# Recurrent mixer of a two-block network: the last pooled tile turned among the last head's units, output tiles in another order, decays and states placed among the running sums, and the opening's row sums moved up

## What the reference computes, cut to what matters

```python
def hgrn2_mixer(q_in, f_in, i_in, g_in, lb, norm_g):
    log_f = logaddexp(log(lbh), log1p(-lbh) + log_sigmoid(z)); k = (1 - lbh) * sigmoid(-z)
    o = hgrn2_chunkwise(q, k, v, log_f)      # S_t = diag(f_t) S_{t-1} + k_t outer v_t, o_t = S_t^T q_t
    o = o * rsqrt(mean(o * o, axis=-1) + EPS) * norm_g
    return o.reshape(B, T, D_A) * silu(g_in)

o_a = hgrn2_mixer(q_a, f_a, i_a, g_a, lb_all[l], hgrn_norm[l])       # features 0 to 511
o_b = multiscale_pool(u_b, pool_w[l], pool_scale[l])                 # features 512 to 1023
x = x + concatenate([o_a, o_b], axis=-1) @ w_out[l]
```

## Time and profile before

| | |
|---|---|
| Time, median of 3 runs | 3008.76 us (3006.59 to 3009.8) |
| The profiled execution, its own time | 3008.41 us |
| Its span in the trace | 3006.6 us |
| TensorE busy in the span | 2968.4 us (99%) |
| VectorE, ScalarE, GpSimd busy | 1636.9, 1124.9, 71.8 us |
| Recurrence of the mixer, layer 1 and layer 2 | 1222.9 to 1289.4 us and 2351.6 to 2417.4 us |

### The profile page before, as it was taken

One profiled execution on the slowest core, in us unless ns is written; L12 is line 12 of the kernel. 1 busy time (PEld: TensorE's weight loads), 2 busy tenths in 40 slices (PEclk: granted clock), 3 DMA queues, 4 the chain that ended last, 5 costly groups with the idle time before them and its releaser, 6 DMA issues.

```text
span 3006.6 us, 33005 instructions
## 1 busy us (share of the span) xinstructions
PE 2968.4 (99%) x14050; PEld 2420.9 (81%) x14050; DVE 1636.9 (54%) x1869; ACT 1124.9 (37%) x1341; POOL 71.8 (2%) x84
## 2 busy tenths in 40 slices
PE   8999999999999999999999999999999999999998
PEld 6786877878888888878788888888888878788886
DVE  5656555565545564654545446545564654545445
ACT  5536445454222235434422223222235434422222
POOL 0000000000000000300000000000000300000000
PEclk9999999999999999999999999999999999999999
DMA  4121221212233232023122222222232014222221
GB/s 157 43 93 55 88 95 43 84 65 97 98 116 111 89 115 98 29 71 140 71 98 98 90 93 98 98 101 96 92 119 98 29 71 140 70 98 98 91 92 69
DMA packets 41922, 270.51 MB, mean 90 GB/s; under 512 B 5776, under 2 KB 6032, under 8 KB 10544
## 3 DMA queue, kind: packets, MB, share of 16 engines
q1 hardware_dynamic: 41776, 268.40, 25.4%
HBM read 266.22 MB, written 2.10 MB: 89 GB/s over the span
## 4 chain that ended last, share of the span: by engine, by line
PE 87%; DVE 7%; ACT 5%; issue 1%; DVEq 0%; POOL 0%; DMA 0%; ACTq 0%; SPq 0%; POOLq 0%
PE PS L257 26%; PE PS L259 25%; PE PS L258 25%; DVE w_lo L231 4%; ACT w_hi L223 3%; DVE XT L1560 2%; PE PS L2175 1%; PE PS L635 1%; PE PS L1149 1%; PE PS L1177 1%; PE PS L2435 1%; PE PS L2466 1%; PE PS L694 0%; PE PS L996 0%; PE PS L2155 0%
## 5 line engine op out<-in xcount | busy, mean ns | idle before, releaser
L223 ACT ACTIVATE w_hi<-w_raw 128x2048 fp32r<-128x2048 f32 x241 | 461.2, 1914 | 1156.8 <-PE PS L259 1156.5
L231 DVE TENSOR_TENSOR w_lo<-w_raw,w_hi 128x2048 fp32r<-128x2048 f32 x239 | 547.7, 2292 | 398.1 <-ACT w_hi L223 397.2
L257 PE MATMUL PS<-uh_b,w_hi 128*128 128x512 f32 x1312 | 511.7, 390 | 0.0
L259 PE MATMUL PS<-uh_b,w_lo 128*128 128x512 f32 x1312 | 510.6, 389 | 0.0
L258 PE MATMUL PS<-ul_b,w_hi 128*128 128x512 f32 x1312 | 510.5, 389 | 0.0
L257 PE MATMUL PS<-uh_a,w_hi 128*128 128x512 f32 x864 | 341.3, 395 | 4.2 <-DVE XT L548 3.4
L258 PE MATMUL PS<-ul_a,w_hi 128*128 128x512 f32 x864 | 336.9, 390 | 0.0
L259 PE MATMUL PS<-uh_a,w_lo 128*128 128x512 f32 x864 | 336.9, 390 | 0.0
L259 PEld LDWEIGHTS PS<-uh_b,w_lo 128*128 128x128 f32 x1312 | 246.2, 188 | 51.3
L257 PEld LDWEIGHTS PS<-uh_b,w_hi 128*128 128x128 f32 x1312 | 246.3, 188 | 51.0
L258 PEld LDWEIGHTS PS<-ul_b,w_hi 128*128 128x128 f32 x1312 | 246.3, 188 | 50.7
(11 more groups left out here) (334 smaller groups left out, 3679.4 us busy)
## 6 DMA issues: line engine op xcount, KB each, us to landing
w_raw<-in_weights SPq DMA_DIRECT2D x241, 1024.0 KB, 4.8
XT<-in_xT SPq DMA_DIRECT2D x8, 256.0 KB, 5.6
mem_raw<-in_mem SPq DMA_DIRECT2D x2, 1024.0 KB, 4.8
out<-XT SPq DMA_DIRECT2D x8, 256.0 KB, 2.0
bands<-in_bands SPq DMA_DIRECT2D x2, 768.0 KB, 6.2
mask_numbers<-in_masks SPq DMA_DIRECT2D x1, 1152.0 KB, 7.6
w_raw<-in_weights SPq DMA_DIRECT2D x4, 256.0 KB, 4.4
p_raw<-in_pT SPq DMA_DIRECT2D x2, 512.0 KB, 3.5
```

The costliest lines, as they stand in the source:

```text
L223: act.activation(self.hi[g % 2][:], self.raw[g % 2][:], ACT.Copy).then_inc(self.hi_done.sem, 1)
L231: dve.tensor_tensor(self.lo[g % 2][:], self.raw[g % 2][:], self.hi[g % 2][:], ALU.subtract).then_inc(self.lo_done.sem, 1)
L257: pe.matmul(out, sh, mh, start=first, stop=False)
L259: return pe.matmul(out, sl, mh, start=False, stop=last)
```

## The change

Four edits, in all of which the same matmuls are issued:

- The turning order becomes 4, 5, 6, 7, 0, 1, 2, 3 with other banks. Tile 7 is turned after unit 2 of the last head, its split is made before the heads' tiles, and the output tiles are multiplied in another order in `finish`.
- VectorE's `finish` of head 2 and the first `invert` move to later places among the last head's units.
- At the head of the recurrence the order on TensorE was four sums, decays, all states; it becomes two sums, decays, a sum, two states, a sum, the third state.
- In the opening `rows.sums` is issued in block 1 before chunk 5's products, and not after the block.

```diff
@@ -564,8 +564,8 @@
 class TurnByTiles(Stage):
 
 
-    ORDER = (4, 5, 6, 0, 1, 2, 7, 3)
-    BANKS = (1, 2, 0, 5, 0, 1, 2, 1)
+    ORDER = (4, 5, 6, 7, 0, 1, 2, 3)
+    BANKS = (1, 2, 5, 0, 0, 1, 2, 0)
 
     def __init__(self, sig, k, src, u, rec):
         self.k, self.src, self.u, self.rec, self.out = k, src, u, rec, None
@@ -596,16 +596,16 @@
 
         for c in (0, 1, 2):
             self.tile(pe, c)
-        self.tile(pe, 7)
+        out.tile(pe, 0, 7)
         pe.wait_ge(*self.rec.outread.at(HH))
-        for c in (4, 5, 6):
-            out.tile(pe, 1, c)
-        for c in (0, 1, 2, 7):
-            out.tile(pe, 0, c)
+        out.tile(pe, 1, 4)
+        out.tile(pe, 0, 0)
+        out.tile(pe, 0, 1)
         self.tile(pe, 3)
-        out.tile(pe, 1, 0)
+        out.tile(pe, 0, 2)
+        out.tile(pe, 1, 5)
         out.tile(pe, 0, 3)
-        for c in (1, 2, 7, 3):
+        for c in (6, 7, 0, 1, 2, 3):
             out.tile(pe, 1, c)
 
 
@@ -1011,9 +1011,15 @@
                 i.then_inc(w.used.sem, 1)
             else:
                 project(0, 0, 0)
-            project(0, 1, 0, (lambda pe, t: self.rows.sums(pe) if t == 1 else None) if g0 else None)
             if g0 == 0:
-                self.rows.sums(pe)
+                def features_and_sums(pe, c):
+                    self.u_ready(pe, c)
+                    if c == 5:
+                        self.rows.sums(pe)
+
+                tokens_block(pe, w, 1, u, 1, lambda t: k.PS[:, t, :], ready=features_and_sums)
+            else:
+                project(0, 1, 0, lambda pe, t: self.rows.sums(pe) if t == 1 else None)
         else:
             project(0, 1, 0)
         if not self.dilated:
@@ -1952,15 +1958,16 @@
         act.wait_ge(*self.dec.at(1))
         act.activation(self.m.dec[:], self.k.PS[:, 4, 0:HH * 2], ACT.Exp).then_inc(self.dec_exp.sem, 1)
 
-    def states(self, pe):
+    def states(self, pe, tiles):
         k, m = self.k, self.m
         pe.wait_ge(*self.suffix_exp.at(4))
         pe.wait_ge(*self.kp.at(3))
-        for c in range(NT - 1):
+        for c in tiles:
             for h in range(HH):
                 cols = slice(h * P, (h + 1) * P)
                 i = pe.matmul(k.PS[:, 5 + c, cols], m.Kp[:, c, cols], m.V[:, c, cols], start=True, stop=True)
-        i.then_inc(self.outer.sem, 1)
+        if NT - 2 in tiles:
+            i.then_inc(self.outer.sem, 1)
 
 
 class Recurrence(Stage):
@@ -2021,6 +2028,8 @@
             if h == 2:
                 for c in (4, 5, 6):
                     self.turn.hi_of(act, c)
+            if h == 3:
+                self.turn.hi_of(act, 7)
             act.wait_ge(*self.out.at(h + 1))
             if h + 2 < HH:
                 exps(h + 2, (0, 1))
@@ -2030,7 +2039,7 @@
                 exps(h + 2, (2, 3))
             if h == 2:
                 self.root(act, 0)
-        for c in (0, 1, 2, 7):
+        for c in (0, 1, 2):
             self.turn.hi_of(act, c)
         self.root(act, 1)
         self.turn.hi_of(act, 3)
@@ -2093,14 +2102,17 @@
                     dve.copy_predicated(AT[:].rearrange("p c t -> p (c t)"), m.masks[:, LEVELS * 256:], k.PS[:, b, :])
                 dve.drain()
                 dve.sem_inc(self.kept.sem, 1)
+                last = h == HH - 1
                 if h and unit == 0:
-                    finish(h - 1)
-                    if h == HH - 1:
-                        self.invert(dve, 0)
+                    if not last:
+                        finish(h - 1)
                     weigh(h, (4, 5))
                 if h and unit == 1:
                     weigh(h, (6,))
-                if h == HH - 1 and unit == 3:
+                    if last:
+                        finish(h - 1)
+                if last and unit == 3:
+                    self.invert(dve, 0)
                     self.turn.lo_of(dve, 6)
 
         def finish(h):
@@ -2125,10 +2137,11 @@
                 self.turn.lo_of(dve, 4)
                 self.turn.lo_of(dve, 5)
             keep(h)
+        self.turn.lo_of(dve, 7)
         self.norm(dve, 0, (0, 1, 2))
         finish(HH - 1)
         self.invert(dve, 1)
-        for c in (0, 1, 2, 7):
+        for c in (0, 1, 2):
             self.turn.lo_of(dve, c)
         self.norm(dve, 1, (3,))
         self.turn.lo_of(dve, 3)
@@ -2188,6 +2201,8 @@
                     self.turn.tile(pe, 5)
                 if unit in (1, 3) and h == 3:
                     self.turn.out.tile(pe, 0, 4 if unit == 1 else 5)
+                if unit == 2 and h == 3:
+                    self.turn.tile(pe, 7)
 
         def outputs(h):
             pe.wait_ge(*self.kept.at(self.UNITS * (h + 1)))
@@ -2206,11 +2221,14 @@
         turn_keys(0)
         pe.wait_ge(*self.states.mapped_read.at(4))
         pe.wait_ge(*self.states.tables_hi.at(2))
-        for c in range(NT):
-            sums(0, c)
+        sums(0, 0)
+        sums(0, 1)
         pe.wait_ge(*self.kcopied.at(1))
         self.states.decays(pe)
-        self.states.states(pe)
+        sums(0, 2)
+        self.states.states(pe, (0, 1))
+        sums(0, 3)
+        self.states.states(pe, (2,))
         turn_keys(1)
         for c in range(NT):
             sums(1, c)
```

## The result

The changed kernel takes 3017.79 us, the median of 9 runs (3013.59 to 3020.14), against 3008.89 us (9 runs) for the kernel before: a ratio of 1.0028, with a 95% interval of 1.002 to 1.0037. The forecast was 3015.8 us. The profiled execution took 3017.43 us, with a span of 3015.7 us; the one of before took 3008.4, so that 9.0 us have to be found in the two traces, where the prediction summed 7.4.

A forecast was written before the change was run, and what follows sets the result against it. TensorE, busy 99% of the span, was taken as the bound. Opening -1.1, head +6.0, clock +13.6 and tail -6.1 and -5.0 sum to +7.4 us on 3008.4: 3015.8 us, range 3010.5 to 3020 (3001.5 to 3021.5 with rivals).

The forecast's parts named there:

- What bounds the kernel: Whole kernel: TensorE is busy 99%, so reordering can only give back, or add, its holes and low-clock time.
- The opening: Block 1 to block 2: the 1.39 us hole for block 2's split goes; -1.1 us.
- the eight one-column matmuls now wait 0.1 to 0.2 us: Opening, block 1 at chunk 5: the moved row sums wait only 0.1 to 0.2 us for the last row sum.
- The head of the recurrence: Before unit 0 of head 0: later fourth exponential delays the state copy; 3.0 us hole per layer, +6.0 us.
- The clock: Head 0's 56 narrow matmuls and the work behind: the hole brings the clock down; 6.8 us a layer, +13.6 us.
- the rival with a short fall: Head 0: clock falls only 3.4 us in each layer, or in one layer alone; 3005.6 us, chance 0.17.
- The tail: Last head to output block 2: three old holes go; -6.1 us in layer 1, -5.0 us in layer 2.
- tile 6's low part: Last head: VectorE has this split at 10.9 us, TensorE wants it at 10.5; a new hole of 0.45 us.
- The sum: Whole kernel: -1.1 + 6.0 + 13.6 - 6.1 - 5.0 = +7.4 us on 3008.4, giving 3015.8 us; chance 0.52.
- the hole opened: Against the rival that unit 0 does not wait for the state copy, so no hole; 2995.2 us, chance 0.06.
- the clock did not hold over it: Against the rival that the clock holds over the hole before unit 0; 3002.2 us, chance 0.13.
- through the whole of head 0: Rival: clock stays low through all of head 0, 9.7 us a layer; 3021.6 us, chance 0.12.

The follow-up runs named there:

- experiment 1: The changed kernel with the head of the recurrence back in the old order (four sums, decays, all states): 2996.79 us, ratio 0.9961.
- Experiment 4: The kernel before with only the edits to the turned tiles and the last head; old opening and front: 2997.17 us, ratio 0.9965.
- experiment 2: The kernel before with only the new order at the head of the recurrence: 3029.23 us, ratio 1.0069.
- experiment 3: The changed kernel plus 12 unread matmuls of 512 columns in the hole before unit 0 of head 0, both layers: 3002.18 us, ratio 0.9979.
- Experiment 7: The changed kernel plus 13 unread fp32 products of one column (26 matmuls) in the hole before unit 0, both layers: 3016.73 us, ratio 1.0022.
- experiment 5: The changed kernel with only the decays before the third sums and all states after the fourth: median 3004.51 us (2999.7 to 3011.59), ratio 0.999.
- experiment 8: The changed kernel with VectorE copying the states after the first two weighings of head 0: 3007.93 us, ratio 0.9998.
- experiment 6: Experiment 1's kernel with the opening's row sums before chunk 7 instead of chunk 5: 2996.48 us, ratio 0.9957.

## Why the prediction was right

**What bounds the kernel.** Right: with TensorE at 99%, all that the change moved was idle time of TensorE and its clock.

**The opening** was mis-sized: -1.1 us forecast. In the profiled execution it is +0.32 - 0.53 = -0.2 us, and experiments 1 and 4 make it -0.4 us by the medians, which their scatter does not tell from none. The step that failed is "the eight one-column matmuls now wait 0.1 to 0.2 us". They waited 0.87 us [the opening's rows above], because VectorE's totals end 17.3 us after the first matmul here, against 16.5 in the earlier trace rows, behind later loads of the input (ScalarE waits 0.98 us for a late chunk, 0.32 before), and because TensorE had one to two slow matmuls less at the start and was there earlier. In experiment 1's execution neither holds (totals at 16.6 us, 14 slow matmuls), the sums don't wait, and the term comes out at 35.52 - 36.45 = -0.9 us. So the working was right for one order of arrival, and both orders occur. The 1.2 us that disappear from the view of waits were not a gain of 1.2 us.

**The head of the recurrence** was right in mechanism and size: 2.95 us measured in layer 1 against 3.0. The chain from the fourth exponential over the seven weighings to the state copy and unit 0 is in the rows as described, with 0.1 us between copy and unit. Undoing it alone (experiment 1) and doing it alone (2) both show it. The price of the delay by runs is 5.4 us for the two layers, forecast 6.0.

**The clock** was right in mechanism and near in size. By the traces, the stretch from unit 0 to the next group of 24 narrow matmuls takes 23.04 us in the changed kernel and 16.53 in experiment 3, 6.5 us more; in layer 2 it is 23.00 against 16.76, 6.2 us more. The forecast was 6.8 each. Its parts hold as well: the clock fell 1.0 and 1.8 us after the restart (forecast 0 to 2.8), the 56 narrow matmuls cost 11.25 - 6.44 = 4.8 us more in layer 1 (forecast 4.5), and the rest is 1.7 us (forecast 2.3). By the runs, the fall costs 15.6 us, 2.9 more than the 12.7 in these two stretches. Of these, 2.0 us are in the two profiled spans (3015.7 - 3001.0 = 14.7), where they lie partly in the opening and partly in steps of 0.07 to 0.08 us spread over stretches that the change doesn't touch. What makes them is open.

The forecast rested on one fall in the trace of before and on the remark that nothing showed a recovery within narrow matmuls. Taking a value near the upper end for that reason was the choice that mattered, and it separated the forecast from the rival with a short fall (3005.6 us): here too the clock came back only in the wider work behind the narrow series. The Trainium skill (TensorE: Matmul & The Clock Gate, Part 1: The HAM clock gate) calls the throttled state the default, which activity releases. The changed kernel agrees so far that in both layers the low clock ended only in the wider work. Experiment 7 adds that a TensorE which the profile shows as busy without a gap can lose its clock too.

**The tail** was right: unit 0 to output block 2 took 33.48 us, where the order counted through in the prediction gives 33.8 (25.6 plus six tiles of 1.36 us), and the gain is 6.3 us in layer 1 (forecast 6.1) and 4.9 in layer 2 (forecast 5.0). The small wait that the prediction put at tile 6's low part (a hole of 0.45 us) is there, with 0.3 us of idle time in layer 1 and 0.7 in layer 2. Experiment 4 gives the tail alone -11.8 us (forecast -11.1).

**The sum.** The forecast's +7.4 us stands against +9.0 between the profiled executions. Of the 1.6 us of difference, the opening explains 0.9 and the first matmul's later start (input that landed 0.5 us later) 0.5; the spread-out steps took 1.2, and the clock and the tail gave back 0.9 and 0.1. So the total is a little closer than its terms, some of whose errors cancel. The terms of the rivals fell with the trace of the changed kernel and experiments 1 to 3: the hole opened, the clock did not hold over it, and it stayed low for longer than 3.4 us, though not through the whole of head 0, whose outputs ran at 1.00.

**What it means for the change.** It is two changes of opposite sign. The turned tiles' new order is worth about 12 us; the new order at the head costs about 21. Leaving the head as it was gives 2996.8 us (or 2996.5 with the row sums before chunk 7), 0.4% under the kernel before, where the whole change is 0.3% above it.

## What to carry to other kernels

Before work is moved ahead of something on the bounding engine, follow what that something releases on the other engines until the bounding engine needs it back: 3.5 us of decays and states moved ahead of one group of sums came back as 2.9 us of idle time in front of a unit that nobody had touched. Price such a hole by what follows it too: ahead of a long series of narrow matmuls, 2.9 us of rest cost 6 to 8 us more at the low clock, and 2.0 us of rest in the middle of that series cost about 3. And where one edit holds several, time them apart; here the best version was the change without one of its parts.

## What the runs showed of the hardware

- **One kernel's executions can fall into groups.** With a hole of 1.6 us before the narrow series they fell into groups 3.8 and 10.8 us above the fastest group (experiment 5), each with its own mean granted clock. With holes of 2.9 us the clock fell in both layers of the profiled executions (the changed kernel and experiment 2), and with 2.0 us too (experiment 8).
- **The falls differed in length.** They lasted 13.6 to 13.7 us where nearly all of 56 narrow matmuls followed, 17 us with the one-column filler ahead of them, and 6.8 us where only the end of the narrow series was left and projections of 512 columns came soon.
- **The start of the kernel is not the same twice.** The number of matmuls at the slow pace after the first one was 13 in the profiled execution of before, 11 and part of a twelfth in that of the changed kernel, and 14, 11, 10, 10, 9, 7, 13 and 7 in those of experiments 1 to 8 in turn. At 0.21 us each this moves the time by up to 1.5 us, more than the whole opening edit. The Trainium skill (TensorE: Matmul & The Clock Gate, Part 1: The HAM clock gate) says that this count varies between runs of one kernel, with 6, 11 and 14 as its examples; these traces agree.
- **Loads move as well:** the first matmul started between 7.14 and 7.67 us in these ten traces.
- **Narrow matmuls slow down almost in full with the clock.** 56 of them are drawn 12.18 us long in experiment 7, where all ran at 0.50, and 6.44 us at 1.00. By the starts, from the first to the matmul behind the last, it is 11.94 and 6.25 us, or 0.213 and 0.112 us each. The prediction's estimates were 0.21 and 0.11.
